# Separate pools of PSUM banks, four difference buffers, and unread products on TensorE in the second block of a two-block transformer

## The reference, cut to what matters

```
# stick-breaking, 8 heads of 64, 128 meta positions ahead of 512 tokens
z = q @ k.T * scale
log_keep = where(valid, log_sigmoid(-z), 0)
log_tail = reverse_cumsum(log_keep) - log_keep
w = where(valid, exp(log_sigmoid(z) + log_tail), 0);   o = w @ v
# gated recurrence, 4 heads of 128, chunks of 128
decay = exp(where(causal, bc[t] - bc[s], -inf))        # bc: running sum of log f
scores = einsum(q, k, decay);   o = scores @ v + (q * exp(bc)) @ state
state  = exp(b_last) * state + (k * exp(b_last - bc)).T @ v
```

## Time and profile before

| | |
|---|---|
| median of 3 runs | 1964.2 us (1962.18 to 1970.22) |
| the profiled execution's own time | 1964.63 us |
| its span, first to last instruction | 1962.9 us |
| mean granted TensorE clock | 0.911 of 2.4 GHz |
| stick-breaking | 1141.2 to 1266.8 us |
| recurrence | 1266.8 to 1351.4 us |
| experts of the second block | 1448.6 us to the end |

### The profile page before, as it was taken

The page is one execution under the profiler, slowest core; times in us unless marked ns, Lnnn a source line. Parts: engine busy times, 40 slices in busy tenths (PEclk is TensorE's granted clock), DMA queues, the critical chain, the costliest instruction groups (busy, mean ns, idle before and its releaser), DMA issues.

```text
span 1962.9 us, 18798 instructions
## 1 busy us (share of the span) xinstructions
PE 1613.7 (82%) x7544; PEld 1076.3 (55%) x7544; DVE 755.9 (39%) x1191; ACT 335.5 (17%) x555; POOL 265.2 (14%) x286
## 2 busy tenths in 40 slices
PE   6997999988988797784799989976968777787873
PEld 4685888766867433331588857866843233332331
DVE  6898655444263311113522258576231000100003
ACT  3301000124002010001201157532100000000001
POOL 0102003200000311102100014553020000000001
PEclk9998999999989799897799967988979999999996
DMA  4221223210417799996112100101779999999993
GB/s 181 74 86 65 86 86 104 68 65 1 150 65 314 262 424 423 425 423 263 71 65 86 65 1 0 44 1 44 287 276 422 427 426 427 427 427 427 428 413 154
DMA packets 53315, 416.21 MB, mean 212 GB/s; under 512 B 11872, under 2 KB 13152, under 8 KB 24944
## 3 DMA queue, kind: packets, MB, share of 16 engines
q1 hardware_dynamic: 43504, 398.22, 50.5%
q0 software_dynamic: 9728, 16.81, 2.3%
HBM read 402.37 MB, written 29.39 MB: 220 GB/s over the span
## 4 chain that ended last, share of the span: by engine, by line
PE 51%; DMA 28%; DVE 11%; ACT 4%; POOL 3%; issue 2%; SPq 0%; POOLq 0%; DVEq 0%; ACTq 0%
PE bank L1217 31%; PE bank L547 7%; DMA arena<-in_expert_down 7%; DMA arena<-in_expert_up 6%; DMA arena<-in_expert_gate 5%; DMA ring<-in_expert_in 5%; PE bank L557 3%; DMA arena<-in_expert_in 2%; DVE arena L1861 1%; PE bank L1471 1%; DMA ring<-in_stream_a 1%; DVE top L1860 1%; DVE ring_low L1756 1%; PE bank L1330 1%; PE bank L1439 1%
## 5 line engine op out<-in xcount | busy, mean ns | idle before, releaser
L547 PE MATMUL bank<-arena 128*64 128x512 f32 x960 | 286.1, 654 | 76.5 <-DMA arena<-in_expert_gate 19.8
L547 PEld LDWEIGHTS bank<-arena 128*64 128x64 f32 x960 | 95.8, 151 | 250.7 <-issue 248.3
L547 PE MATMUL bank<-ring,arena 128*64 128x512 f32 x576 | 187.3, 640 | 24.8 <-DMA ring<-in_expert_gate 10.1
L714 DVE TENSOR_TENSOR arena<-misc,bank 128x256 f32<-128x256 f32 (+1 forms) x32 | 17.7, 554 | 450.7 <-PE bank L547 307.9
L1755 DVE CAST ring_high<-ring 128x2048 fp32r<-128x2048 f32 x60 | 76.4, 1274 | 292.2 <-DMA ring<-in_stream_a 169.9
L1756 DVE TENSOR_TENSOR ring_low<-ring,ring_high 128x2048 fp32r<-128x2048 f32 x60 | 140.8, 2346 | 2.1
L557 PE MATMUL bank<-arena 128*64 128x512 f32 x480 | 123.2, 603 | 22.0 <-issue 9.8
L1217 PE MATMUL bank<-ring_low,xn_high 128*128 128x512 f32 x288 | 113.7, 395 | 0.0
L1217 PE MATMUL bank<-ring_high,xn_low 128*128 128x512 f32 x288 | 113.0, 392 | 0.0
L1217 PE MATMUL bank<-ring_high,xn_high 128*128 128x512 f32 x288 | 112.9, 392 | 0.0
L547 PEld LDWEIGHTS bank<-ring,arena 128*64 128x64 f32 x576 | 61.4, 147 | 91.2 <-issue 91.2
(11 more groups left out here) (354 smaller groups left out, 2969.0 us busy)
## 6 DMA issues: line engine op xcount, KB each, us to landing
ring<-in_stream_a SPq DMA_DIRECT2D x42, 1024.0 KB, 5.0
arena<-in_expert_in SPq DMA_DIRECT2D x20, 2048.0 KB, 33.8
arena<-in_expert_gate SPq DMA_DIRECT2D x20, 2048.0 KB, 28.7
arena<-in_expert_up SPq DMA_DIRECT2D x20, 2048.0 KB, 28.2
arena<-in_expert_down SPq DMA_DIRECT2D x20, 2048.0 KB, 29.0
ring<-in_expert_in SPq DMA_DIRECT2D x12, 2048.0 KB, 33.6
ring<-in_expert_up SPq DMA_DIRECT2D x12, 2048.0 KB, 31.6
ring<-in_expert_down SPq DMA_DIRECT2D x12, 2048.0 KB, 30.4
```

What stands on the lines that cost most here:

```text
L547: last = nc.tensor.matmul(h[side * SLOTS:(side + 1) * SLOTS, :], tokens[:, k, side * SLOTS:(side + 1) * SLOTS], w[:, k * 512:(k + 1) * 512 ...
```

## The change

1. **Pools of banks.** A unit may name a set of banks and takes them in turn. Z gets banks 0 to 2, R banks 3 to 6, SO bank 7. All other units still take the eight in turn.
2. **|z|** becomes max(-z, z) (`scalar_tensor_tensor` with z as both inputs) in place of the integer mask.
3. **Four difference buffers** instead of two, and a deeper order: ScalarE takes exp(n + 2) at level n, VectorE does products(n), then read(n - 2), GpSimd may be four levels ahead. `head_exps` is split into `chunk_exps` (levels 4 and 5) and `query_exp` (level 3). `head_out` of the last head moves from level 1 to level 2. GpSimd's four output jobs are spread over levels 4, 6, 0 and 1 of two heads.
4. **Unread products.** `keep_busy(b, times)` writes products of `sums_left` and a part of the loaded `wo2` weights, 128 x 512, into the bank that the next unit will overwrite: 6 ahead of each SO, 4 ahead of each level. `begin2` moves ahead of the wait for the operands, so that the bank is free first. TensorE also waits once for that part of the weights to be split.

```
@@ class Units
+    def add(self, key, reader, banks=tuple(range(BANKS))):
+        turn = self.turn.get(banks, 0)
+        self.turn[banks] = turn + 1
+        self.place.append(banks[turn % len(banks)])
...
+        earlier = [n for n in range(i) if self.place[n] == self.place[i]]
@@ second_block_units
-                u.add(("Z", h, s), "dve")
+                u.add(("Z", h, s), "dve", (0, 1, 2))
-                u.add(("R", h - 2, s), "dve")
+                u.add(("R", h - 2, s), "dve", (3, 4, 5, 6))
-            u.add(("SO", h - 3), "act")
+            u.add(("SO", h - 3), "act", (7,))
-            if lv == 1 and h >= 1:
+            if lv == 2 and h >= 1:
                 u.add(("HO", h - 1), "act")
@@ TensorE
+            pe.wait_ge(weights_split, 2 * (len(STREAM1) + n_stream2["wo2_0"]) + 1)
+            def keep_busy(b, times):
+                w = ring_parts[2 * (len(STREAM1) + n_stream2["wo2_0"]) % RING][0]
+                for i in range(times):
+                    nc.tensor.matmul(b[:, :], sums_left[:, 1, :], w[:, i % (KC // 2), :], start=True, stop=True)
...
+                    b = begin2(("SO", g))
+                    keep_busy(b, 6)
                     pe.wait_ge(weight_ready, g + 1)
-                    b = begin2(("SO", g))
...
+                    b = begin2(("L", h, lv))
+                    keep_busy(b, 4)
                     pe.wait_ge(level_ready, n + 1)
-                    b = begin2(("L", h, lv))
@@ ScalarE
-                    if lv == LEVELS - 1 and h + 1 < HGH:
-                        head_exps(h + 1)
-                    if n + 1 < HGH * LEVELS:
-                        level_exp(n + 1)
+                    if n + 2 < HGH * LEVELS:
+                        level_exp(n + 2)
...
-                    if lv == 1 and h >= 1:
+                    if lv == 2 and h >= 1:
                         head_copy(h - 1)
+                    if lv == 3 and h + 1 < HGH:
+                        query_exp(h + 1)
+                    if lv in (4, 5) and h + 1 < HGH:
+                        chunk_exps(h + 1, range(2 * lv - 8, 2 * lv - 6))
@@ VectorE
-                    V.tensor_scalar(v.bitcast(U32), z.bitcast(U32), 0x7FFFFFFF, None, ALU.bitwise_and).then_inc(z_ready, 1)
+                    V.scalar_tensor_tensor(v, z, -1.0, z, ALU.mult, ALU.max).then_inc(z_ready, 1)
...
+                if n >= 2:
+                    dve.wait_ge(psum_filled2, U2.filled(("L", (n - 2) // LEVELS, (n - 2) % LEVELS)))
                 level_products(n)
-                if n >= 1:
-                    level_read(n - 1)
+                if n >= 2:
+                    level_read(n - 2)
@@ GpSimd
-                if n >= 2:
-                    pool.wait_ge(level_ready, n - 1)
+                if n >= DIFFS:
+                    pool.wait_ge(level_ready, n - DIFFS + 1)
...
+                if h >= 1 and lv == 4:
+                    out_square(h - 1)
+                if h >= 1 and lv == 6:
+                    out_root(h - 1)
+                if h >= 2 and lv == 0:
+                    out_scale(h - 2)
+                if h >= 2 and lv == 1:
+                    out_gate(h - 2)
+            out_scale(HGH - 2)
+            out_gate(HGH - 2)
```

More of the change, by code:

```diff
@@ L93, in __init__ @@
     def __init__(self):
-        self.index, self.reader = {}, []
-    def add(self, key, reader):
+        self.index, self.reader, self.place, self.turn = {}, [], [], {}
+    def add(self, key, reader, banks=tuple(range(BANKS))):
         assert key not in self.index, key
+        turn = self.turn.get(banks, 0)
+        self.turn[banks] = turn + 1
         self.index[key] = len(self.reader)
         self.reader.append(reader)
+        self.place.append(banks[turn % len(banks)])
     def bank(self, key):
-        return self.index[key] % BANKS
+        return self.place[self.index[key]]
     def filled(self, key):
@@ L113, in read_before @@
     def read_before(self, key):
-        old = self.index[key] - BANKS
-        if old < 0:
+        i = self.index[key]
+        earlier = [n for n in range(i) if self.place[n] == self.place[i]]
+        if not earlier:
             return None, 0
+        old = earlier[-1]
         who = self.reader[old]
@@ L1675, in level_exp, with chunk_exps, query_exp @@
                 act.wait_ge(diff_ready, n + 1)
-                v = diff[:, n % 2, :] if n % LEVELS < LEVELS - 1 else diff[:, n % 2, 1:SEQ:2]
+                v = diff[n % DIFFS] if n % LEVELS < LEVELS - 1 else diff[n % DIFFS][:, 1:SEQ:2]
                 A.activation(v, v, ACT.Exp).then_inc(diff_exp, 1)
-            def head_exps(h):
+            def chunk_exps(h, chunks):
+                for t in chunks:
+                    ins = A.activation(kd[:, h % 2, t * P:(t + 1) * P], bc[:, h, t * P:(t + 1) * P], ACT.Exp,
+                                       bias=bc[:, h, (t + 1) * P - 1:(t + 1) * P], scale=-1.0)
+                if t == NT - 1:
+                    ins.then_inc(kd_exp, 1)
+            def query_exp(h):
                 if h >= 2:
                     act.wait_ge(psum_filled2, U2.filled(("HO", h - 2)))
[L1682 to L1685, removed]
                 A.activation(qexp[:, h % 2, :], bc[:, h, P:L2], ACT.Exp).then_inc(q_exp, 1)
@@ L1691, in head_copy @@
                              b[:, :].rearrange("p (t d) -> p t d", d=HD)))
-            head_exps(0)
+            chunk_exps(0, range(NT))
             level_exp(0)
+            query_exp(0)
+            level_exp(1)
             for h in range(HGH):
@@ L2068, in level_products @@
                 dve.wait_ge(diff_exp, n + 1)
-                e = halves(diff[:, n % 2, :], half)
+                e = halves(diff[n % DIFFS], half)
                 ins = V.tensor_tensor(halves(qE[:, n % 2, :], half)[:, :, 1, :], e[:, :, 1, :],
@@ L2257, in level_diff, with head_rows, out_square, out_root @@
                 ins.then_inc(diff_ready, 1)
+            def head_rows(g):
+                return mixed[:, :, 512 + g * HD:512 + (g + 1) * HD], rstd[:, 32 + 4 * g:36 + 4 * g]
+            def out_square(g):
+                wait_read2(pool, ("HO", g))
+                v, _ = head_rows(g)
+                G.tensor_tensor(out_squares, v, v, ALU.mult).then_inc(squared, 1)
+            def out_root(g):
+                pool.wait_ge(squares_ready, SBH + g + 1)
+                then(root_of(head_rows(g)[1], HD))
+            def out_scale(g):
+                v, root = head_rows(g)
+                then(G.tensor_tensor(v, v, root[:, :, None].broadcast_to([P, NT, HD]), ALU.mult))
+            def out_gate(g):
+                v, _ = head_rows(g)
+                G.tensor_tensor(v, v, hgate[:, :, g * HD:(g + 1) * HD], ALU.mult).then_inc(heads_normed, 1)
             pool.wait_ge(psum_filled2, U2.filled(("SO", SBH - 1)))
```

18 lines of the change are left out of this document (5 added, 13 removed).

## The result

The changed kernel took 1991.4 us, the median of four runs (1985.23 to 1993.86); the kernel before took 1964.13, also of four. The ratio is 1.0131, with a 95% interval of [1.0109, 1.0153]: slower, and above the range of the prediction. The profiled execution took 1993.86 us with a span of 1991.8, 28.9 more than before, at the same mean clock of 0.911.

What follows compares the result with a forecast made beforehand. Neither stick-breaking nor the recurrence has a full engine at a full clock; a saving there passes on whole. 1964.63 + 6.4 (|z| and pools) + 3.3 (tail) - 11.5 (recurrence) = 1962.8, given as 1962 us, range 1947 to 1975.

Steps and rivals of the forecast that it cites:

- |z|: Stick-breaking, each round: the new operation takes 1.99 us against 1.09, +0.9, and if blocked ends 1.99 after GpSimd's end.
- rival B: Stick-breaking: the new |z| is not blocked by GpSimd; 1949 us in all, faster, chance 0.2.
- five rounds of eight: Stick-breaking: |z| blocked in rounds 1 and 2 and three of rounds 3 to 7, at 14.7 us each.
- The tail's +3.3: End of stick-breaking: unread products ahead of two SOs, 2 x 1.37, plus 0.5 us waiting for ScalarE's copy of SO.
- The waits that I named: Stick-breaking, TensorE: stops at Z(h, 3) and R(h, 4) for VectorE's reads; 2 to 3 us idle at R's fifth unit.
- VectorE's waits for the exp of a level: Recurrence: 14.4 us, 8 times, before the change; VectorE was to be free of them after it.
- the rounds: Stick-breaking, rounds 1 to 7: five at 14.7 and two at 12.5 us, 98.5 against 93.0, +5.5.
- A: Whole kernel, the forecast itself: the terms cancel; 1962 us, own range 1951 to 1972, chance 0.55.
- C: Stick-breaking: the clock falls after TensorE's idle time, 7 us a fall; 1969 us with one, 1976 with two, chance 0.15.
- D: Recurrence: gives little back as the shared port works badly, 19.5 us a head, 78; 1970 us in all, chance 0.1.
- The recurrence: After stick-breaking, four heads: exps two levels ahead cover `head_out` and norm jobs; 17.5 us a head, 70 us, -11.5.
- Ahead of stick-breaking: Everything before the first read of Z: no change, 0 us.

Runs made afterwards that it cites:

- e7: The kernel before with the unread products alone, eight banks in turn, old recurrence order: 1966.02 us, ratio 1.0007.
- e13: The changed kernel with GpSimd's 1792-wide subtraction cut in four pieces: 1973.72 us, ratio 1.0027 to the kernel before.
- e3: The changed kernel without the pools, all units in the eight banks in turn: 1974.54 us, ratio 1.0049 to the kernel before.
- e4: The kernel before with the new recurrence alone (four difference buffers, deeper order), no pools, integer mask, no unread products: 1968.58 us, ratio 1.0004.
- e8: The kernel before with the new recurrence alone, its chunk exps moved a level earlier and GpSimd's norm jobs later: 1955.31 us, ratio 0.9956.
- e6: The kernel before with the pools of banks alone (Z three, R four, SO one): 1976.47 us, ratio 1.0065.
- e9: The kernel before with GpSimd's 1792-wide subtraction cut in four pieces of 448: 1960.13 us, ratio 0.9974.
- e14: The kernel before with the pools of banks and GpSimd's subtraction cut in four pieces: 1961.4 us, ratio 0.9971.

## Why the prediction was wrong

**Right.** |z| costs 0.9 us more and, as an operation with two inputs, is blocked (so rival B was out); a blocked one ends one length of itself after GpSimd; five rounds of eight are blocked, and the race is decided by 0.12 us. The tail's +3.3 at full clock is near e7's +3.2, though one part of it is another there. The waits that I named did come, at Z(h, 3) in rounds 1 to 3 and at R(h, 4): 2.72 and 2.56 us, inside my "2 to 3", but in two of the blocked rounds only (in round 3 it was 0.43). VectorE's waits for the exp of a level vanished.

**The step that failed first: the rounds, +10.3 us.** I had kept apart as rivals what came together: A's five blocked rounds, C's fall of the clock and D's 78 us of recurrence are all in this one execution. A had TensorE idle for 2 to 3 us in each blocked round; C was a fall of the clock, at 0.15, with "they come right behind it" against it. The fall follows from A's own idle time: it comes right behind the 2.72 and the 2.56 us, and in e13, the same kernel with short races, both these idle times and the falls behind them are absent. Without VectorE's waits for Z behind that fall, the five blocked rounds are 75.0 us (I had 73.5) and the other two 23.9 (25.0). The waits make up 9.9 more: 5.10 us ahead of Z's first read, 1.8 within the reads of that round (4.5 us in place of 2.7), and 2.96 a round later, when the clock is up again but TensorE is still behind. That is nearly the whole miss. That the two free rounds fit is luck: I had them set by TensorE's 12.5 us, and they were 11.6 us, and 12.3 with the held |z|. The waits of VectorE for R in this stretch, 1.04 and 0.96 us, cost nothing, as they lie beside ScalarE's exp and log, which take 4.8 us there as in every round. The kernel before had such waits too, 7.0 us behind its fall at 1209, and they stood in the 93.0 that I compared with. My forecast had them gone; the changed kernel has 9.9. The unread products ahead of SO stand behind the idle time in TensorE's list, so they couldn't cover it, as I had written myself and then not priced. e3 shows the source of this idle time: without the pools it is gone, and 0.39 us of the waits for Z are left.

**The tail, +6.3 us.** I costed it at full clock and from the last head's R on. That part is right: from R's start to the end of the last SO it takes 14.2 us (1283.29 to 1297.50) against 11.0 (1255.44 to 1266.42), +3.2. My 0.5 us for the wait for SO's copy had no row behind it; it measured 0.46. What I left out is when TensorE gets to that R. Before, it began 6.7 us after round 7's end, held by GpSimd's low part; now it begins 12.6 after (1270.66 to 1283.29), held by TensorE itself: +6.0. The chain shows why. The second fall of the clock, at 1264.51, makes the SO and the R ahead of it longer by 5.87 - 3.07 and 5.98 - 4.51, 4.3 us in all, the unread products by 0.5 (1.98 against 1.44), and the next six are 1.44 more, 6.3 in all. Without them GpSimd's low part, done at 1277.30, would have held R again. The last 0.4 is a longer operation of VectorE (L2140, 1.15 against 0.72) behind the last SO.

**The recurrence, +8.8 us.** The step that failed is the sentence that the exps, two levels ahead, cover `head_out` and the norm jobs. They cover them for VectorE's products. They don't for GpSimd, which reaches the square of the norm before ScalarE's copy is there and waits with the next differences behind it, nor for VectorE's wait for the chunk exps, which the change moved next to the end of the head. I had summed each engine's busy time and let them mesh. e4 excludes the unread products, |z| and the banks as the cause, and e8 shows that these waits, taken together, were: 70.8 us, with the same buffers and the forecast of 70.

**Ahead of stick-breaking, +5.2 us.** I had this at nothing, since nothing there is changed. Its cause stays open; the last section has what the runs show.

**How the parts add.** On the kernel before, |z| alone costs 9.3 us of stick-breaking, the pools 10.1, the unread products -1.3: 18.0 of the 26.3 that all three cost. The other 8.3 come from their company. I read it so, without a run for it: |z| is longer when it is blocked, the pools lay TensorE idle for that time, and the unread products are load in a chain that runs at half clock. Taken out of the changed kernel, they give back 10.7, 20.3 and 14.3.

## What to carry to other kernels

When a forecast holds an idle time of an engine that has a clock to lose, price the lower clock in the same case, and everything that follows it, instead of in a rival. Where VectorE and GpSimd meet on SBUF, first cut GpSimd's instruction in pieces: it made the race for the lock nearly harmless (|z| at most 1.81 us in place of 4.57) and took 8 us off this stage, more than any other edit of it; the whole is at 0.9974. For a deeper pipeline look at each engine's in-order list for the one job that waits for something late; the four buffers gave at most 2.4 us until such jobs were moved, and 10.6 after.

## What the runs showed of the hardware that I had not expected

**A race of 0.12 us decides over 3 to 4 us,** and edits on other engines flip it: the short |z| won by 0.13 in the kernel before and lost by 0.12 in e6, whose only edit is TensorE's choice of banks, because Z's reads took 0.25 us longer.

**The lock is held for one instruction.** Four instructions of 448 columns in a row on GpSimd leave |z| at 1.1 to 1.8 us (e9), where it took up to 4.57 behind one of 1792 columns.

**Code that isn't changed ran later.** All fifteen changed kernels reach stick-breaking later than the kernel before, by 1.2 to 8.8 us, also e9, whose edit comes into play only at 1163. About 3 us of it come in the first block, between 320 and 480 us, where TensorE waits longer for GpSimd ahead of transposes. By 434 us e9 is 3.2 us later than the kernel before, and by 485, where a group of eight products takes 3.68 us instead of 2.40 at a lower clock, 4.6. By waits from 321 to 485 us, the kernel before:

```profile
PE bank L1209 <- POOL arena L2194: 3.8, 4, 1.7
```

and e9, the same four waits:

```profile
PE bank L1209 <- POOL arena L2194: 5.9, 4, 3.8
```

In e7 and e14 this wait is no longer than before (2.9 and 3.8 us), and their start is only 1.5 and 1.2 us later. The medians carry it too: against their batch's kernel before they are 2.4 to 6.5 us worse than the cuts of the profiles say, fifteen times of fifteen (e9: cuts -9.7, median -6.4). All fifteen are held against one profile of the kernel before, though, and an execution of that one that was early at this place would show the same. Whether the place of the code in memory or something else decides it wasn't tried and stays open. It also bounds what this case can say: differences under some 5 us between medians of two kernels are read here from the cuts.
